# Expert weights of a mixture-of-experts layer loaded in 2 MB transfers made of 16 KB pieces

## The reference

```
hdn = x @ w1 + b1
gt  = minimum(hdn[:, :1024], 7);  up = clip(hdn[:, 1024:], -7, 7)
act = (up + 1) * gt * sigmoid(1.702 * gt)
acc = acc + g[:, None] * (act @ w2 + b2)
```

## Time and profile before

| what | value |
|---|---|
| median of three executions | 1314.96 us |
| profiled execution, its own time | 1311.35 us |
| its span, first to last instruction | 1309.6 us |
| around the span | 1.75 us |
| TensorE busy, share of the span | 1174.1 us, 90% |
| VectorE, ScalarE, GpSimd busy | 27%, 13%, 7% |
| mean granted TensorE clock | 0.970 of full speed |
| bytes read from HBM | 436.65 MB |
| bulk queue's packets, share of the span of 16 DMA engines | 82.2% |

### The profile page before, as it was taken

The page is one execution under the profiler, slowest core; times in us unless marked ns, Lnnn a source line. Parts: engine busy times, 40 slices in busy tenths (PEclk is TensorE's granted clock), DMA queues, the critical chain, the costliest instruction groups (busy, mean ns, idle before and its releaser), DMA issues.

```text
span 1309.6 us, 14918 instructions
## 1 busy us (share of the span) xinstructions
PE 1174.1 (90%) x5551; PEld 546.2 (42%) x5551; DVE 353.8 (27%) x693; ACT 171.9 (13%) x330; POOL 95.4 (7%) x211
## 2 busy tenths in 40 slices
PE   3997888999999999999899998999998999999875
PEld 2754566533433343334334333433343343334264
DVE  6799823212111111121211111111212111111133
ACT  2113322110011001010100100100011001100022
POOL 4674400000000000000000000000000000000000
PEclk9997889998999999999999999999999999997988
DMA  8413033299999999999999999999999999999600
GB/s 298 148 40 158 11 131 129 79 418 418 417 394 417 418 416 417 417 417 419 418 418 417 419 418 418 417 417 417 417 418 419 417 419 416 419 416 417 279 1 34
DMA packets 89189, 438.56 MB, mean 335 GB/s; under 512 B 13632, under 2 KB 16832, under 8 KB 55344
## 3 DMA queue, kind: packets, MB, share of 16 engines
q1 hardware_dynamic: 88528, 437.60, 82.2%
q10 hardware_dynamic: 624, 0.45, 0.1%
HBM read 436.65 MB, written 2.41 MB: 335 GB/s over the span
## 4 chain that ended last, share of the span: by engine, by line
PE 64%; DMA 12%; DVE 10%; SPq 7%; ACT 4%; issue 3%; ACTq 0%; DVEq 0%
PE ps L926 24%; PE ps L943 14%; DMA ring_up<-in_w_up_dram 11%; PE ps L910 7%; SPq L397 4%; SPq L404 3%; PE ps L804 2%; PE ps L1065 2%; PE ps L518 2%; PE ps L921 2%; PE ps L933 1%; ACT region L1258 1%; PE ps L598 1%; PE ps L869 1%; DVE region L1720 1%
## 5 line engine op out<-in xcount | busy, mean ns | idle before, releaser
L926 PE MATMUL ps<-ring_up,region 128*64 128x512 f32 x2112 | 463.5, 594 | 5.5 <-DMA ring_up<-in_w_up_dram 5.4
L926 PEld LDWEIGHTS ps<-ring_up,region 128*64 128x64 f32 x2112 | 147.3, 137 | 319.4 <-issue 296.9
L943 PE MATMUL ps<-ring_dn,region 128*64 128x512 f32 x1056 | 242.1, 612 | 22.7 <-ACT region L1258 22.7
L1716 DVE TENSOR_SCALAR region<-ps 128x512 f32<-128x512 f32 x33 | 22.8, 692 | 718.4 <-PE ps L926 718.4
L943 PEld LDWEIGHTS ps<-ring_dn,region 128*64 128x64 f32 x1056 | 74.7, 140 | 169.1 <-issue 138.3
L910 PE MATMUL ps<-region,n_tok 128*128 128x256 f32 (+1 forms) x384 | 95.8, 394 | 0.0
L1256 ACT ACTIVATE region<-region 128x512 f32<-128x512 f32 x33 | 20.8, 631 | 497.8 <-DVE region L1716 497.8
L869 PE MATMUL ps<-region 128*128 128x264 f32 (+1 forms) x272 | 69.4, 399 | 15.0 <-DVE fb L1711 12.4
L485 POOL COPY region<-kst 128x64 f32 (+1 forms) x33 | 7.9, 239 | 1020.5 <-PE ps L926 956.0
L910 PEld LDWEIGHTS ps<-region,n_tok 128*128 128x128 f32 (+1 forms) x384 | 67.3, 188 | 31.2 <-issue 24.2
L1268 ACT ACTIVATE region<-ps 64x512 f32<-64x512 f32 x66 | 39.1, 592 | 245.8 <-PE ps L943 245.4
(11 more groups left out here) (347 smaller groups left out, 823.5 us busy)
## 6 DMA issues: line engine op xcount, KB each, us to landing
ring_up<-in_w_up_dram SPq DMA_DIRECT2D x264, 1024.0 KB, 19.1
ring_dn<-in_w_down_dram SPq DMA_DIRECT2D x132, 1024.0 KB, 17.9
ring_up<-in_w_in_dram SPq DMA_DIRECT2D x4, 1280.0 KB, 10.5
ring_dn<-in_w_out_dram SPq DMA_DIRECT2D x1, 4096.0 KB, 25.4
ring_up<-in_w_ple_gate_dram SPq DMA_DIRECT2D x4, 1024.0 KB, 11.5
x_tok<-in_x_prompt_dram SPq DMA_DIRECT2D x2, 512.0 KB
ring_up<-in_w_glu_dram SPq DMA_DIRECT2D x1, 1024.0 KB, 15.3
region<-in_w_ple_proj_dram SPq DMA_DIRECT2D x1, 1024.0 KB
```

Source lines behind the costliest of these rows:

```text
L926: m = mm(ps[64 * (q % 2):64 * (q % 2) + 64, HID_B + q // 2, :], xe[:, k, slots], ring_up[:, k, q * 512:(q + 1) * 512], start=False, stop=( ...
L943: m = mm(ps[64 * half:64 * half + 64, OUT_B, :], act_t[:, f % 4, 64 * (f // 4):64 * (f // 4) + 64], ring_dn[:, f, 512 * half:512 * half + ...
```

## The change: what it does, and the diff

Two rows of up weights go to a partition in one transfer, rows 256k+2p and 256k+2p+1, which are neighbours in HBM: one piece of 16 KB, 128 pieces and 2 MB per transfer, four transfers per expert. Four rows of down weights go to a partition, rows 512s+4p to 512s+4p+3: again one piece of 16 KB, 128 pieces and 2 MB, two transfers per expert. SyncE waits until both up rows (four down rows) of a transfer are released, and TensorE waits for both (all four) before it uses the first.

With that, slot 2k+j holds the rows 256k+2p+j, so `gather` takes every second column of `n_tok` as its stationary operand (`x_cols`, a step of 8 bytes), `turn_activations` every fourth column of `act_v` (`act_cols`, a step of 16 bytes), and the norm's weights for `xe` are needed in the new order: they are loaded into a new tile `g_xe` with 512 pieces of 8 bytes. Of expert 0 row 4 is now issued with row 5, after `embedding_loads`.

```diff
@@ buffers and views
+        g_xe = sb("g_xe", [P, KD])
+        x_cols = n_tok[:].rearrange("t c (k p j) -> t c k j p", p=P, j=2)
+        act_cols = act_v.rearrange("p (q j) -> p j q", j=4)
-        up_in = [sem(f"up_in{k}") for k in range(UP)]
-        dn_in = [sem(f"dn_in{k}") for k in range(DN)]
+        up_in = [sem(f"up_in{k}") for k in range(UP // 2)]
+        dn_in = [sem(f"dn_in{k}") for k in range(DN // 2)]
@@ SyncE, after b_down's load (and 64 -> 80 in the three waits on ld_router)
+            sp.dma_start(g_xe[:].rearrange("p (k j) -> p k j", j=2),
+                         A["norm_ffn"][0].rearrange("(k p j) -> p k j", p=P, j=2)).then_inc(ld_router, 16)
@@ SyncE, the expert weights
-            up_w = A["w_up"][0].rearrange("e (k p) n -> e k p n", p=P)
-            dn_w = A["w_down"][0].rearrange("e (s k p) n -> e s p k n", p=P, k=2)
+            up_w = A["w_up"][0].rearrange("e (k p j) n -> e k p j n", p=P, j=2)
+            dn_w = A["w_down"][0].rearrange("e (s p k) n -> e s p k n", p=P, k=4)
 
             def expert(e, t, first=False):
-                for k in range(UP):
-                    if first and k == 5:
+                for k in range(UP // 2):
+                    if first and k == 2:
                         embedding_loads()
                     if first:
-                        sp.wait_ge(*((Z["q_ps"], 6) if k < 5 else (Z["glu_ps"], KM) if k == 5 else (Z["s5_free"], 1)))
+                        sp.wait_ge(*((Z["q_ps"], 6) if k < 2 else (Z["glu_ps"], KM) if k == 2 else (Z["s5_free"], 1)))
                     else:
-                        sp.wait_ge(Z["up_free"], t * UP + (k + 1 - UP))
-                    sp.dma_start(ring_up[:, k], up_w[bass.ds(e, 1), k].rearrange("e p n -> (e p) n")
+                        sp.wait_ge(Z["up_free"], t * UP + (2 * k + 2 - UP))
+                    sp.dma_start(ring_up[:, 2 * k:2 * k + 2], up_w[bass.ds(e, 1), k].rearrange("e p j n -> (e p) j n")
                                  ).then_inc(up_in[k], 16)
-                for s in range(DN):
+                for s in range(DN // 2):
                     if first:
                         sp.wait_ge(Z["mix_ps"], KD)
                     else:
-                        sp.wait_ge(Z["dn_free"], t * DN + (s + 1 - DN))
-                    sp.dma_start(ring_dn[:, 2 * s:2 * s + 2], dn_w[bass.ds(e, 1), s].rearrange("e p k n -> (e p) k n")
+                        sp.wait_ge(Z["dn_free"], t * DN + (2 * s + 2 - DN))
+                    sp.dma_start(ring_dn[:, 4 * s:4 * s + 4], dn_w[bass.ds(e, 1), s].rearrange("e p k n -> (e p) k n")
                                  ).then_inc(dn_in[s], 16)
@@ TensorE: gather (and gather_visit alike), up, turn_activations, down
-                               n_tok[0:nt, c, k * P:(k + 1) * P], sel[0:nt, c].rearrange("p a s -> p (a s)"),
+                               x_cols[0:nt, c, k // 2, k % 2], sel[0:nt, c].rearrange("p a s -> p (a s)"),
...
-                    pe.wait_ge(up_in[k], 16 * t + 16)
+                    if k % 2 == 0:
+                        pe.wait_ge(up_in[k // 2], 16 * t + 16)
...
-                    m = tr(ps[:, TURN_B, j * P:(j + 1) * P], act_v[:, j * P:(j + 1) * P], ident)
+                    m = tr(ps[:, TURN_B, j * P:(j + 1) * P], act_cols[:, j], ident)
...
-                    if f % 2 == 0:
-                        pe.wait_ge(dn_in[f // 2], 16 * t + 16)
+                    if f % 4 == 0:
+                        pe.wait_ge(dn_in[f // 4], 16 * t + 16)
@@ VectorE: gathered (and gathered_visit alike)
-                                    col(vecs[:, V_FFN + 2 * b:V_FFN + 2 * b + 2], QC), ALU.mult
+                                    col(g_xe[:, 2 * b:2 * b + 2], QC), ALU.mult
```

More of the change, by code:

```diff
@@ L819, in _ @@
             pe.wait_ge(Z["norm_sb"], 12)
-            pe.wait_ge(ld_router, 64)
+            pe.wait_ge(ld_router, 80)
             for k in range(KD):
@@ L1002, in gather_visit @@
                     for c, (t0, nt) in enumerate(CHUNKS):
-                        m = mm(ps[:, 4, k * C:(k + 1) * C], n_tok[0:nt, c, k * P:(k + 1) * P], sel[0:nt, c, 0],
+                        m = mm(ps[:, 4, k * C:(k + 1) * C], x_cols[0:nt, c, k // 2, k % 2], sel[0:nt, c, 0],
                                start=(c == 0), stop=(c == 2))
@@ L1627, in _ @@
             dve.wait_ge(Z["lg_ps"], 2)
-            dve.wait_ge(ld_router, 64)
+            dve.wait_ge(ld_router, 80)
             groups = ((slice(0, 2), P), (slice(2, 3), NB))
@@ L1765, in gathered_visit @@
                 V.tensor_tensor(xe[:, :, 0:C], ps[:, 4].rearrange("p (k s) -> p k s", k=KD),
-                                col(vecs[:, V_FFN:V_FFN + KD], C), ALU.mult).then_inc(Z["xe_rdy"], 1)
+                                col(g_xe[:], C), ALU.mult).then_inc(Z["xe_rdy"], 1)
             def visit(v, e):
```

## The result

The changed kernel is slower: a median of 1318.13 us over 8 runs (1316.14 to 1320.93) against 1314.91 us over 8 runs of the kernel before; the ratio is 1.0035, with a 95% interval of 1.0019 to 1.0051. The forecast was 1305.2 us, faster. The profiled execution after has a span of 1319.0 us and a mean granted clock of 0.953; before it was 1309.6 us and 0.970.

A forecast was written before the change was run, and what follows sets the result against it. Transfers bound the loop before, TensorE the whole loop after: -12.4 us for the last gather, +2.6 for strided loads, sum -9.8, so 1314.96 becomes 1305.2 us. The range was 1300 to 1317.

The forecast's parts named there:

- What bounds the kernel: Expert loop before: TensorE sets the pace first, 117.5 us a quad, then the transfers, 120.5, once their lead is spent.
- the transfers: Weight loads in the expert loop: 16 KB pieces reach 428.3 GB/s, a quad takes 117.5 us instead of 120.5.
- Granularity: Up weights in the expert loop: waiting for two rows per transfer adds 3.9 us, once, to the transfers' line.
- Other edits on the queue: SyncE's queue: moving row 4 of expert 0, loading the norm's weights and halving the issues change nothing.
- Strided weight loads: Stepped stationary operands on TensorE: nothing for the gather, 0.08 us per expert for the transposes, 2.6 us over 33 visits.
- The transposes pay in full: Rival, between activation and down matmuls: loads of 252 ns, 0.66 us per visit, +9.5 us in all, 1324.5; chance 0.09.
- two strided rivals: Stepped loads slow TensorE: in the transposes, +9.5 us, 1324.5, chance 0.09; or in the gather, +16, 1331, chance 0.08.

The follow-up runs named there:

- up weights alone: Only the up weights as changed (2 MB, 16 KB pieces, stepped gather), down weights and transposes as in the kernel before: 1308.76 us, ratio 0.9953.
- 2 MB transfers with the old pieces: The kernel before with 2 MB transfers and coarser waits, but rows, pieces (8 and 4 KB) and transposes as before: 1318.8 us, ratio 1.0025.
- plain turns: The changed kernel with one edit taken back, the transposes read 128 neighbouring columns again (part of the result wrong): 1302.95 us, ratio 0.993.

## Why the prediction was wrong

**What bounds the kernel, and the transfers: right.** The line through two piece lengths gave 428.3 GB/s, and 428 to 429 were measured at a piece that no row had shown; with it TensorE became the bound of the whole loop, as forecast. The up weights alone gave 1308.76 us against 1309 from the same rates.

**Granularity: right.** 3.3 us (ratio 1.0025, interval 1.2 to 5.5 us) for 3.9.

**Other edits on the queue:** nothing was found to pay; the transfers of expert 0 are not in the chain after. One reading there was wrong: SyncE's issues were on the chain before, 7% of it by the page. After there are none, but fewer issues were not the gain, since the 2 MB transfers with the old pieces have as few and are slower.

**Strided weight loads: the size was right, the step failed.** Reading at half speed was priced at +63 ns per load; it was +64. I took 0.08 us per visit, and the turn grew by 0.09. That these agree is partly luck: by the prediction's own sum +63 ns would have cost 0.159 us per visit, and 0.08 was the halfway value. The gather paid next to nothing (196 for 189 ns, 11.99 for 11.92 us). What failed is the step from there to the time: "times 33 visits: 2.6 us", added to a TensorE line of "7 x 117.54". It supposed that TensorE's pace is the sum of its instructions at the clock that the stretches showed, 1.00; a fall of the clock was no term at all. But the clock fell more often behind the longer turn, and with work in the turn it did not. The missing term is seven slow down stages x 1.69 us = 11.8 us on TensorE's line in the profiled execution, where the loads themselves cost 33 x 0.09 = 3.0 us.

**The last quad: a smaller term left out.** With plain turns six quads took 117.60 us each, but the seventh, from 1055.51 to 1177.02, took 121.51. In 2.40 us there TensorE and VectorE select the further visits, and `up` waits for it. That stood in the trace before too (the down stage ends at 1079.31 + 7.09 = 1086.40, the next `up` begins at 1088.80), but under the transfers' bound. And a stretch of `up` at the lower clock took 15.61 instead of 13.91 us. So from the first gather to the last plain turns took 827.1 us and before 835.2: 8.1 us gained in the loop, not 12.4. By the ratio 0.993 the gain is 9.2 us (5.9 to 12.5).

With both terms the loop after comes out: 7 x 117.54 + 11.8 + 28 x 0.09 for the turns between these gathers + 2.4 = 839.5 us; from 356.87 to 1196.40 are 839.5, 4.3 more than before (the 0.07 us of each gather are left out). From the ratios, 1.0035 with the step and 0.993 without are 1.05% apart, 13.8 us; in the profiled loops it is 839.5 - 827.1 = 12.4.

**The rivals.** "The transposes pay in full" came out on the right side, at less than half its price (+9.5 us for the whole; 3.2 by the medians, 4.6 by the ratio), and by another mechanism: a load takes 209 ns, and its reading did not grow to 252. Its point of decision, 0.38 us per visit, was crossed: (11.8 + 3.0) / 33 = 0.45. The sign that the prediction gave for the strides came too: gathers more than 118.5 us apart without a landing, and transposes' loads past 200 ns. By the rule of the Trainium skill ("Advanced Engine Details and Errata", section "SBUF Cachelines") a step of 8 bytes should be free, one of 16 bytes not. Here the transposes' loads take 207 ns at 8 bytes and 209 at 16: the measurement agrees with the page at 16 bytes, differs from it at 8 bytes, and decides. In the gather 8 bytes cost 7 ns.

Two slips in the numbers changed nothing: at 410 GB/s the quads of 122.8 us give +20 us, not +19, and the 0.16 for slower is less than the 0.09 and 0.08 of the two strided rivals that make it up.

**What I could have seen.** In the first quad before, one down stage took 9.46 us instead of 7.09, and the clock of the stretch around it was 0.97:

```profile
297.88 9.46 PE ps L943 x32
```

The clock had already fallen around a turn, and once more at 1011.92. Those were the rows to ask how much room the turn has.

In the profiled execution after, the first gather of the loop is 5.5 us later than before (356.87 for 351.38). That is not put down to the change: over the kernels here it lies between 348.5 and 359.3 us. Plain turns, with the same transfers, have it at 349.91, and the latest is that of the 2 MB transfers with the old pieces and old transposes.

## What to carry to other kernels

Where a faster transfer makes TensorE the bound, price the pauses of TensorE along with its instructions: an edit of 0.1 us in a pause can cost 1.7 us of half clock behind it, and the granted clock before and after that pause is the row to look at. If the pause can't be shortened, a matmul into a bank that is about to be overwritten can hold the clock; here that cost nothing that could be measured (ratio 1.0003 on the kernel before). Lengthen the pieces of a transfer before its total size: from 1 to 2 MB, in this stream, the rate followed the piece alone.

## What the runs showed of the hardware

- In this stream the rate was 410 GB/s with pieces of 4 KB, 421 to 422 with 8 KB, 428 to 429 with 16 KB. An estimate from the first two, 9 ns and 36.8 ps per byte for a piece on each of the 16 engines, gave 428.3 for the third. 2 MB transfers of the short pieces stayed at 418.
- A transpose's stationary operand of 128 x 128 32-bit floats loads in 145 ns from neighbouring columns and in 207 to 209 ns from every second or every fourth; a matmul's (the gather's), of the same size, in 189 ns from neighbouring columns and in 196 from every second.
- VectorE's product of 128 x 512 takes 692 ns with a contiguous destination and 1037 ns where neighbouring elements go 512 bytes apart.
- TensorE's clock fell to its lower level, at 1.69 us a time, behind turns of 4.34 and 4.41 us in five of six quads of the changed kernel. Between 310 and 1070 us it did not behind turns of 4.26 us in four kernels, it did behind 4.32 us three times in 24, and it never did behind a turn with added matmuls of 0.6 us in its pauses.
